# A two-layer streaming encoder on one core: the last group's down projection as seven block products, and the entry's evictions and weights ahead of the operand's forming

## The reference, cut to what matters

```python
D_MODEL, D_FF = 1024, 2816

def rmsnorm(x, g):
    y = x * lax.rsqrt(jnp.mean(x * x, axis=-1, keepdims=True) + EPS)
    return y * g

def half_swiglu(x, g, w_gu, w_down):
    h = rmsnorm(x, g) @ w_gu
    a, b = jnp.split(h, 2, axis=-1)
    return x + 0.5 * ((jax.nn.silu(a) * b) @ w_down)
```

## Time and profile before

| | us |
|---|---|
| median of 3 runs | 2795.7 (2793.03 to 2796.23) |
| the profiled execution | 2792.98 |
| its span | 2791.4 |
| PE busy in the span | 2745.6 (98%) |
| DVE busy | 1918.0 (69%) |
| ACT busy | 1205.5 (43%) |
| POOL busy | 191.1 (7%) |
| granted TensorE clock, mean | 0.997 |

### The profile page before, as it was taken

One profiled execution on the slowest core, in us unless ns is written; L12 is line 12 of the kernel. 1 busy time (PEld: TensorE's weight loads), 2 busy tenths in 40 slices (PEclk: granted clock), 3 DMA queues, 4 the chain that ended last, 5 costly groups with the idle time before them and its releaser, 6 DMA issues.

```text
span 2791.4 us, 47466 instructions
## 1 busy us (share of the span) xinstructions
PE 2745.6 (98%) x18946; PEld 2698.7 (97%) x18946; DVE 1918.0 (69%) x2687; ACT 1205.5 (43%) x1625; POOL 191.1 (7%) x190
## 2 busy tenths in 40 slices
PE   8999999999999999999999999999999999999997
PEld 8999999999999999999999999999999999999997
DVE  7788864646364677888657788864555567888755
ACT  5454443323232444454444454444434443545443
POOL 0000003101011110000010000002000020000021
PEclk9999999999999999999999999999999999999998
DMA  3322323333233313223321222323222112232231
GB/s 120 91 81 85 97 76 126 102 111 110 94 108 98 101 57 95 85 81 93 93 76 57 88 76 89 93 78 119 94 83 90 68 59 68 82 94 83 86 95 57
DMA packets 80908, 246.96 MB, mean 88 GB/s; under 512 B 8464, under 2 KB 25120, under 8 KB 79680
## 3 DMA queue, kind: packets, MB, share of 16 engines
q1 hardware_dynamic: 71408, 204.67, 23.5%
q0 software_dynamic: 9296, 39.40, 4.0%
HBM read 226.74 MB, written 17.30 MB: 87 GB/s over the span
## 4 chain that ended last, share of the span: by engine, by line
PE 94%; DVE 4%; ACT 1%; issue 1%; DMA 0%; ACTq 0%; SPq 0%; DVEq 0%
PE ps L615 42%; PE ps L544 32%; PE ps L927 7%; PE ps L803 4%; PE ps L980 2%; PE ps L596 1%; PE ps L901 1%; PE ps L1014 1%; DVE xn L1763 1%; PE ps L964 1%; PE ps L868 1%; PE ps L852 0%; PE ps L1000 0%; DVE w_lo L1724 0%; PE ps L871 0%
## 5 line engine op out<-in xcount | busy, mean ns | idle before, releaser
L1083 ACT ACTIVATE w_hi<-raw 128x1024 fp32r<-128x1024 f32 (+2 forms) x210 | 201.3, 959 | 516.6 <-PE ps L544 376.8
L1724 DVE TENSOR_TENSOR w_lo<-raw,w_hi 128x1024 fp32r<-128x1024 f32 (+2 forms) x210 | 236.8, 1128 | 93.9 <-ACT w_hi L1083 91.1
L544 PE MATMUL ps<-x_hi,w_hi 128*128 128x320 f32 x1216 | 284.3, 315 | 14.4 <-DVE x_lo L1729 8.9
L544 PE MATMUL ps<-x_lo,w_hi 128*128 128x320 f32 x1216 | 277.5, 309 | 0.0
L544 PE MATMUL ps<-x_hi,w_lo 128*128 128x320 f32 x1216 | 277.5, 310 | 0.0
L544 PEld LDWEIGHTS ps<-x_hi,w_hi 128*128 128x128 f32 x1216 | 203.9, 188 | 19.8 <-DVE w_lo L2466 8.9
L1147 ACT ACTIVATE wx_hi<-raw 128x1024 fp32r<-128x1024 f32 (+1 forms) x96 | 96.6, 1006 | 258.4 <-PE ps L615 226.2
L544 PEld LDWEIGHTS ps<-x_lo,w_hi 128*128 128x128 f32 x1216 | 203.8, 188 | 0.0
L544 PEld LDWEIGHTS ps<-x_hi,w_lo 128*128 128x128 f32 x1216 | 203.8, 188 | 0.0
L615 PE MATMUL ps<-x_hi,wx_hi 128*128 128x320 f32 x576 | 178.2, 309 | 3.0 <-DVE wx_lo L1821 3.0
L615 PE MATMUL ps<-x_hi,w_hi 128*128 128x320 f32 x576 | 178.7, 310 | 0.0
(11 more groups left out here) (310 smaller groups left out, 7696.8 us busy)
## 6 DMA issues: line engine op xcount, KB each, us to landing
raw<-wst SPq DMA_DIRECT2D x292, 512.0 KB, 3.6
raw<-wst SPq DMA_DIRECT2D x96, 384.0 KB, 3.2
raw<-wst SPq DMA_DIRECT2D x32, 256.0 KB, 2.6
s<-st_d POOLq DMA_DIRECT2D x8, 1024.0 KB, 5.1
sts_o<-s POOLq DMA_DIRECT2D x16, 512.0 KB, 3.4
rd<-dec_d POOLq DMA_DIRECT2D x8, 640.0 KB, 5.6
kc<-kc_d POOLq DMA_DIRECT2D x8, 512.0 KB, 4.4
vc<-vc_d POOLq DMA_DIRECT2D x8, 512.0 KB, 5.2
```

The costliest lines, as they stand in the source:

```text
L544: last = nc.tensor.matmul(out[:, h, :], a, b[:, HALF * h:HALF * (h + 1)], start=start and q == 0, stop=stop and q == 2, skip_group_check=True)
L1083: nc.scalar.activation(w_hi[:, (c["n"] + m) % 2, 0:cols], raw[:, r, 0:cols], ACT.Copy).then_inc(s_whi, 1)
L1724: tt(w_lo[:, p, 0:cols], raw[:, r, 0:cols], w_hi[:, p, 0:cols].bitcast(F), ALU.subtract).then_inc(s_wlo, 1)
```

## The change

It has two halves. **Last group:** SEVEN_DOWN becomes (1, 2, 3), the plain loop goes, and piece 3 does its down projection in four "dn" jobs. With them move feed_hi, feed_lo, the squares and the split of p: fed(old) stands inside the next job behind hi34, squares 0 and 1 in the job for out = 4, squares 2 to 4 in the last job behind the first split of the next phase's weights, squares 5 to 7 after everything. The squares get buffers of their own (sq_mix, sq_ple), as g_lo is now used to its end. **Entry:** normed moves from j = 1, 2 to j = 2, 3, t_sum to j = 4, 5, t_low to j = 6 and d = 0 to 4, the operand's high parts (operand) one j later. And job 1 of piece 1 gets its two weight blocks by hi1, hi2, lo1, lo2 in place of hi12, lo12, its product 1 waiting for the first alone (`alone`).

```diff
--- before.py
+++ after.py
@@ -47,7 +47,7 @@
...
-SEVEN_DOWN = (1, 2)
+SEVEN_DOWN = (1, 2, 3)
 B11, T1, B21, T2, T3, B22, T4 = range(7)
@@ -251,6 +251,12 @@
...
             sq = sb("sq", [P, 2, TOK], F, s)
+        with ExitStack() as s:
+            sb("over_t_hi2", [P, 3, 4, HALF], F, s)
+            sq_mix = sb("sq_mix", [P, 2, TOK], F, s)
+            sb("over_t_mid", [P, 3 * 4 * HALF - 4 * TOK], F, s)
+            sq_ple = sb("sq_ple", [P, 2, TOK], F, s)
         with ExitStack() as s:
@@ -431,6 +437,12 @@
...
+        def squares(norm):
+            if norm == 0 or norm > len(phases) - 1 or phases[norm - 1] != "ffn":
+                return sq
+            return sq_ple if phases[norm] == "ple" else sq_mix
@@ -455,15 +467,18 @@
...
+            alone0 = c["fast"] // N_FAST * (1 + len(SEVEN_DOWN))
             pair0 = (c["fast"] // N_FAST * len(SEVEN_DOWN) + SEVEN_DOWN.index(piece)) * 3 if seven else None
...
                          f=c["g"] + sum(PIECES[:piece]) + i, par=i % 2, k=i // 2, odd=i % 2,
-                         pair=pair0 + i // 2 if seven else None,
+                         pair=pair0 + i // 2 if seven else None, alone=alone0 if piece == 1 and i == 1 else None,
                          first=i == 0, last=i == FAST[piece] - 1, **banks(c, i)) for i in range(FAST[piece])]
...
                               sum=pair0 // 3 * (KT // 2) + i,
+                              alone=alone0 + 1 + SEVEN_DOWN.index(piece) if i == 1 else None,
                               f=c["g"] + sum(PIECES[:piece + 1]) - 1, pair=pair0 + 2,
@@ -471,7 +486,7 @@
...
             jobs = fast_pairs(c, piece)
-            nxt = fast_pairs(c, piece + 1)[0] if piece in SEVEN_DOWN else None
+            nxt = fast_pairs(c, piece + 1)[0] if piece < LAST else None
             old = fast_pairs(c, piece - 1)[-1] if piece - 1 in SEVEN_DOWN else None
@@ -665,8 +680,8 @@
...
                             pe.wait_ge(s_glo, CREDIT + d["f"])
-                        if old and old["kind"] == "dn" and old["first"]:
-                            pe.wait_ge(s_lo1, CREDIT + d["pair"] // 3 + 1)
+                        if d["alone"] is not None:
+                            pe.wait_ge(s_lo1, CREDIT + d["alone"] + 1)
                         else:
@@ -742,14 +757,6 @@
...
                                     tiles(g_hi), tiles(g_lo))
-                    if nf_at != LAST:
-                        m += KT
-                        continue
-                    with pe.Fori(0, KT // 4) as i:
-                        for j in range(4):
-                            step(m + j, i, 4)
-                            project(c, m + j, i, 4, (c["unit"] + 1 + m + j) % 4, [(k, k) for k in range(nf)],
-                                    tiles(g_hi), tiles(g_lo), ready if j == 0 else None)
                     m += KT
@@ -1091,7 +1098,7 @@
...
                 act.wait_ge(s_ssum, CREDIT + c_fed + d - 1)
-                nc.scalar.activation(sq[:, d % 2, :], x[:, d, :], ACT.Square).then_inc(s_sq, 1)
+                nc.scalar.activation(squares(norm)[:, d % 2, :], x[:, d, :], ACT.Square).then_inc(s_sq, 1)
@@ -1222,6 +1229,16 @@
...
+                def fed(d):
+                    act.wait_ge(s_up, CREDIT + 2 * d["sum"] + 2)
+                    feed_hi(c["norm"] + 1, d["out"])
+                    act.wait_ge(s_free, CREDIT + o + d["m"] + 2)
+                    feed_hi(c["norm"] + 1, d["out"] + 1)
+                def square_of(n):
+                    square(c["fed"] + KT, c["norm"] + 1, n, s_xhi, c["fed"] + KT + n + 1)
@@ -1239,8 +1256,10 @@
...
                         if not old:
+                            hi1(new)
                             snap2(d)
-                        if new:
+                            hi2(new)
+                        elif new:
                             hi12(new)
@@ -1252,6 +1271,14 @@
...
                             ghi(made)
+                        if piece == LAST and d["kind"] == "dn":
+                            fed(old)
+                            if d["out"] == 4:
+                                square_of(0)
+                                square_of(1)
+                                if c["split_p"]:
+                                    act.wait_ge(s_p, 16 * (c["ple"] + 1))
+                                    nc.scalar.activation(p_hi[:], p_raw[:], ACT.Copy).then_inc(s_phi, 1)
                         if d["kind"] == "gu":
@@ -1260,10 +1287,13 @@
...
                             split_hi(c, d["m"], 0, 0, c["fill"] + d["m"])
+                            for n in range(2, 5):
+                                square_of(n)
                     if piece == LAST:
-                        silu(d)
                         split_hi(c, d["m"] + 1, 0, 0, c["fill"] + d["m"] + 2)
-                        ghi(d)
+                        fed(d)
+                        for n in range(5, KT):
+                            square_of(n)
@@ -1287,9 +1317,9 @@
...
                                     split_hi(c, j, 0, 0, c["fill"] + j + 1)
-                            if j == 3:
+                            if j == 4:
                                 operand(5, 4 * layer + 1, s_t)
-                            if j == 4:
+                            if j == 5:
                                 operand(7, 4 * layer + 2, s_t)
@@ -1305,7 +1335,7 @@
...
                     for d in range(KT):
-                        if nf_at < LAST and d >= KT - 2:
+                        if d >= KT - 2:
                             if d == KT - 2:
@@ -1313,11 +1343,6 @@
...
                         split_hi(c, m + d, 0, 0, c["fill"] + m + d + 1)
-                        if nf_at == LAST:
-                            feed(c["fed"] + KT, c["norm"] + 1, d, s_free, o + m + d + 1)
-                            if c["split_p"] and d == 4:
-                                act.wait_ge(s_p, 16 * (c["ple"] + 1))
-                                nc.scalar.activation(p_hi[:], p_raw[:], ACT.Copy).then_inc(s_phi, 1)
                     m += KT
@@ -1591,10 +1616,10 @@
...
                         pool.wait_ge(s_ss, CREDIT + norm)
-                        nc.gpsimd.tensor_copy(ssum[:], sq[:, 0, :]).then_inc(s_ssum, 1)
+                        nc.gpsimd.tensor_copy(ssum[:], squares(norm)[:, 0, :]).then_inc(s_ssum, 1)
                     else:
                         pool.wait_ge(s_ssum, CREDIT + fed + d)
-                        nc.gpsimd.tensor_tensor(ssum[:], ssum[:], sq[:, d % 2, :], ALU.add).then_inc(s_ssum, 1)
+                        nc.gpsimd.tensor_tensor(ssum[:], ssum[:], squares(norm)[:, d % 2, :], ALU.add).then_inc(s_ssum, 1)
@@ -1822,7 +1847,7 @@
...
                 def lo1(d):
-                    dve.wait_ge(s_hi1, CREDIT + d["pair"] // 3 + 1)
+                    dve.wait_ge(s_hi1, CREDIT + d["alone"] + 1)
                     w = slice(0, d["width"])
@@ -1956,17 +1981,29 @@
...
                             c11_c12(summed)
-                            s1_s2(new)
-                            s3(new)
+                            if new:
+                                s1_s2(new)
+                                s3(new)
                             c21(summed)
-                            lo12(new)
-                            s4(new)
+                            if new:
+                                lo12(new)
+                                s4(new)
                             lo34(d)
+                            if piece == LAST and d["kind"] == "dn":
+                                feed_lo(c["fed"] + KT, c["norm"] + 1, summed["out"])
+                                feed_lo(c["fed"] + KT, c["norm"] + 1, summed["out"] + 1)
+                                if c["split_p"] and d["out"] == 4:
+                                    dve.wait_ge(s_phi, CREDIT + c["ple"] + 1)
+                                    tt(p_lo[:], p_raw[:], p_hi[:].bitcast(F), ALU.subtract).then_inc(s_plo, 1)
                             continue
...
                             s3(new)
-                            lo12(new)
+                            if old:
+                                lo12(new)
+                            else:
+                                lo1(new)
+                                lo2(new)
                         if made:
@@ -1986,11 +2023,11 @@
...
                         split_lo(c, d["m"], 0, 0)
-                        c12(d)
-                        gated(d, 1)
-                        gated(d, 0)
+                        c11_c12(d)
+                        c21(d)
+                        feed_lo(c["fed"] + KT, c["norm"] + 1, d["out"])
                         split_lo(c, d["m"] + 1, 0, 0)
-                        glo(d)
+                        feed_lo(c["fed"] + KT, c["norm"] + 1, d["out"] + 1)
@@ -2023,21 +2060,18 @@
...
                                    ALU.subtract).then_inc(s_glo, 1)
-                            if j in (1, 2):
-                                for n in range(4 * j - 4, 4 * j):
+                            if j in (2, 3):
```

(27 more changed lines are left out.)

## The result

| | before | after |
|---|---|---|
| median, us | 2795.7 (2792.6 to 2796.6) | 2800.9 (2800.2 to 2803.6) |
| ratio | | 1.0024 (95% 1.0015 to 1.0034) |
| span of the profiled execution | 2791.4 | 2798.9 |
| PE busy | 2745.6 | 2736.3 |
| DVE busy | 1918.0 | 2032.2 |

The account below looks back on a forecast made before the run. It took TensorE, busy 2745.6 of 2791.4 us, as the bound. Terms -21.2 - 5.4 - 3.6 + 1.3 + 18.7 + 2.9 gave -7.3, so a median of 2788.4 against 2795.7; range 2776 to 2802.

Parts of the forecast that it names:

- Step 1: Last group's down projection: seven products instead of the plain loop save matmuls, 5.29 us per FFN, -21.2 in all.
- steps 1 to 4: Matmuls saved, entry waits and wx_lo waits removed, and the new snap2 wait, together -28.9 us.
- Steps 2 and 3: FFN entries: six waits for low weights go, -5.4 us; job 1's four waits for wx_lo go, -3.6.
- Step 4: Piece 3's new first "dn" job: a wait for snap2, 0.32 us in starts per FFN, +1.3 in all.
- Step 5: End of the FFN: late squares and six GpSimd adds make TensorE wait for ssum, +18.7 us, bounds 12.5 and 25.
- the dearer rival: End of the FFN: GpSimd and VectorE slow each other, TensorE waits, clock falls further: +7.6 us, 2803.3; chance 0.14.
- Step 6: TensorE's clock falls after long waits: 1.1 us each ple, 0.7 ret, 0 sb; +2.9, bounds 0 and 6.

Follow-up runs that it names:

- experiment 5: The changed kernel with GpSimd's seven adds behind each FFN over 64 of 640 columns, so statistics are wrong: 2768.9 us, ratio 0.9906.
- 3: The changed kernel with 34 extra matmuls ahead of TensorE's wait for ssum in the two ple phases: 2794.5 us, ratio 1.0003.
- experiment 7: experiment 4 with p split one job earlier and, before ple, squares 6 and 7 ahead of the last feeds on ScalarE: 2780.2 us, ratio 0.9951.
- experiment 4: The changed kernel with squares 2 and 3 moved ahead on ScalarE, behind snap1 of the last group's last job: 2788.3 us, ratio 0.9979.
- experiment 1: The kernel before with the entry's half of the change alone: 2784.9 us, ratio 0.9969.
- experiment 8: experiment 7 with the adds of squares 6 and 7 before ple on VectorE instead of GpSimd: 2786.8 us, ratio 0.9971.
- 11: The changed kernel with GpSimd's copy of square 0 and add of square 1 held until the last job's lo56: 2795.9 us, ratio 1.0005.
- 12: experiment 7 with GpSimd's add of square 2 held until the last job's lo56: 2776.6 us, ratio 0.9935.

## Why the prediction was wrong

**Step 1 was right.** The matmuls are gone and worth what I said: by the 7.67 of experiment 5's FFN 1, steps 1 to 4 come to what I summed for them.

**Steps 2 and 3 were right**, 8.7 against 9.0. **Step 4** too: 12 waits of 0.16 instead of 8.

**Step 5, my +18.7, was the first failure.** The waits that the changed kernel adds at the end of the FFN, counted in starts (shown idle plus 0.16), are 1.3 + 1.2 + 6.0 before each ple, 0.6 + 3.6 + 0.5 before ret, and 0.6 + 0.6 + 0.8 + 4.0 before sb beyond what it had: 27.8 against my 18.7, beyond even the upper bound of 25. Of the 9.1 that my sum lacked, 4.2 are before the two ples, 3.7 before sb and 1.2 before ret. It went wrong at three places.

- "Squares 5 to 7 are made in time for their adds" let me leave ScalarE's list out of the sum. I did not follow square 4: it waits 2.0 for the buffer that add 2 frees, and the split of weights and both last feeds are queued behind it. By this x_hi 6 is late, and VectorE idles 2.0 for it. That is the smaller part of what makes x_lo 7 late: the feed, the split and the feed behind it are 0.7, 1.4 and 1.3 longer than alone, 3.4 together.
- In ret and sb I asked only when ssum is due, 48 matmuls after E. x_lo 7 is due before that, in ret after 42 matmuls (the last six use it) and in sb after 21. In both phases TensorE's longest wait is for x_lo 7 (3.4 and 3.85), and I had none. So in sb I had 2.4 where it is 6.1.
- I had the stretching of VectorE by the adds as the dearer rival, as one instruction of 0.88 growing to 2.20 in one place, with a chance of 0.14. The trace before shows adds beside feeds at nearly every output tile, but there the feed starts first and keeps its 0.88, while the add takes 1.64 to 2.08. I took this 2.05 for the price of being side by side. Which of the two pays depends on which starts first, and at the end of the changed FFNs that is mostly the add, so VectorE pays: the last feeds take 1.60 and 2.15, the last split 2.57, p_lo 2.83.

Before ple the wait for ssum is 6.0 where I had 6.4 - 1.7 = 4.7. The chain takes 12.6 from the start of add 2 to its end, where I took 11.3, within my bounds of 9.8 and 12.9. snap1 is 1.3 where I had 1.4; the 1.2 for lo56 I had only in the rival.

**Step 6 was the second.** I took 2.9 for the clock from the earlier trace rows, where a stretch of 3.4 us cost 1.5. I made the stretches no longer than that one. Behind waits of 5.8 the half clock lasted 10.2 us, three times as long, and 3 measures its price at 3.9 and 3.3, where I had 1.1 each. sb, for which I had nothing, had 6.8 us of it: the 27 matmuls from the end of its wait to the sum of squares take 6.41 there and 4.06 in experiment 7, 2.4 more. ret's 3.4 us cost 1.3 by the same comparison with experiment 4 (from the sum of squares to the wait for rstd, 11.01 and 9.69). So the clock took 10.9 in all where I had 2.9.

Added up, -28.9 + 27.8 + 10.9 is +9.8. Against that, the profiled execution lacks 2.1 us of waits in the middle of ret that the one before has (for x, 1.6 before and 1.3 after, and issue, 2.7 and 1.0), and the 1.5 for the half clock of the earlier trace rows. That leaves +6.2 of the span's +7.5, and 1.3 us that I can't place. Whether the change removed that stretch in ret or chance did, no run tells; it is back in experiment 1 and experiment 8.

**The rival.** The slower side had the right mechanism, in part: GpSimd and VectorE hold each other up, lo56 is late by it, and the clock falls in ret and sb too. Its sum of 2803.3 is near the measured time partly by luck, as it has neither the late square 4 nor x_lo 7 in it, and less of the clock than there was. It was to decide once steps 5 and 6 cost more than 34.5 together; they came to 35.6 by the ratio and 34.1 by the medians, so just there. I held it unlikely since I priced the stretch at one instruction per FFN, although three such instructions of VectorE (four before ple) stand there beside the adds.

The Trainium skill's GPSIMD Engine Reference (1, Specifications) says that GpSimd's SBUF interfaces are shared with VectorE and that they contend where a VectorE instruction has two SBUF inputs. The runs agree: splits and feeds with both inputs in SBUF that start while an add runs take up to 3.5 times as long (0.55 became 1.92), and evictions with one input in PSUM keep their 0.81. Had I read that rule beside VectorE's list instead of the factor of two in section 4.1, it would have marked p_lo, two feeds, lo56 and the split at once.

**What stays open.** Why the half clock after the second ple's wait lasted 6.8 us in 11 and 10.2 in the changed kernel, behind the same wait of 5.8, no run tells. Likewise ret's lasted 6.8 in 3 and 11 and 3.4 in the changed kernel, behind the same wait of 3.4. So the length differs between executions, and my prices are those of single ones. How TensorE's waits for x_lo 7 divide between the late x_hi 6 and the longer feeds and split was not tested; experiment 4 shrinks both. The remaining 8 us between 12 and 5 were not taken apart.

## What to carry to other kernels

When an edit moves a step of one engine beside another engine's work, look at the pair and not at each alone: an elementwise add on GpSimd is nearly free beside evictions from PSUM, but feeds and subtractions of VectorE from SBUF to SBUF that start beside it are held up, here to about twice their time. A chain that is drained at the end of a phase should not start late; here two squares a few lines further up were worth 12.6 us. And where it has time in hand, its adds can be put beside evictions: holding a copy and an add back behind one instruction of VectorE was worth 5.3. And a long unbroken wait of TensorE is to be priced with its clock: each of the two of 5.8 cost 3.3 to 3.9 beyond itself.
